# FFN up-projection with the tokens stationary, turned out of PSUM by VectorE; taps and residual sums in other steps

## The chip, the cores and the metric

The program runs on one core of one Trainium2 chip. The metric is the device time of one execution in microseconds (us). The kernel before takes 2447.81 us, the median of three runs (2447.76 to 2447.81).

## The reference, cut to what matters

Two transformer blocks follow each other; the change lies in the feed-forward part of the first. For 256 tokens, D_MODEL 2048 and D_FF 5632, it is

```python
h2 = rmsnorm(x, ffn_norm_w[l])
up = causal_dwconv(h2 @ w_ffn_up[l], conv_w[l], conv_b[l])
a, b = jnp.split(up, 2, axis=-1)
x = x + (jax.nn.silu(a) * b) @ w_ffn_down[l]

def causal_dwconv(u, w, b):          # CONV_WIDTH = 3, along the tokens
    up = jnp.pad(u, ((0, 0), (CONV_WIDTH - 1, 0), (0, 0)))
    y = b
    for j in range(CONV_WIDTH):
        y = y + w[j] * up[:, j:j + S]
    return y
```

The convolution runs along the tokens, feature by feature, and the second product sums over the features.

## The kernel before, in words

All weights come as one stream, w_stream, of some 840 groups in a fixed order. A group is 256 rows by 512 columns of some weight matrix, 512 KB in float32, kept as two 128-row slices of 512 columns. Four slots (RING = 4) hold groups. For each group SP issues a DMA into RAW; ACT copies it rounded into WH ("hi", L1101); DVE subtracts, WL = RAW - WH ("lo", L1605); and PE multiplies. Activations are held as such pairs too, so a product has three terms: hi by hi, lo weight by hi activation, hi weight by lo activation. ACT may write WH of group p+4 when PE has used group p, and SP may refill a slot of RAW when DVE has made its lo.

Each engine's program is written out by hand in the order of the groups. **Step p** on ACT or DVE is: the split of group p+4, then the other work given to that step (`if p == ...`). So the split in step p can begin when PE is through with group p, and everything else that a step holds comes behind its split and ahead of the next.

The feed-forward part takes D_FF in 11 blocks (FB) of 512 features. A block has an "a" tile (its silu branch, 8 groups), a "b" tile (8 groups) and the down-projection of the block before (8 groups, in 4 chunks c of 512 output columns, 2 groups each). The first a and b tiles stand ahead of the loop; the loop over b has 10 passes of 24 groups in the order a, b, down (steps 0 to 23); then come 8 groups of another product (mem1) and the last down-projection.

Up-projection before (`ffn_up`, L876): the weights are the stationary side, 128 columns at a time, and the transposed activations HT (feature rows, hi and lo side by side, 2 x 256 tokens) move. Per group there are 8 matmuls of 512 columns (L892: WH against hi and lo) and 8 of 256 columns (L897: WL against hi). The result has features on partitions: bank f of PSUM holds 128 features by 256 tokens twice, and the two halves are still to be summed. ACT copies one half to FC (`up_copy`, L1365), DVE adds the other and writes FU (`up_sums`, L1902), behind two zero columns. Then the taps, on DVE: a multiply and add of bias (L1911), two multiply-adds (L1913, L1915), each waiting for the one before through `link`. ACT takes silu of the a tile (L1369); for the b tile DVE multiplies the two (`b_tile`, L1921). ACT and DVE make hi and lo of that product, ACTT (`block_hi`, L1375; `block_lo`, L1927); the down-projection needs them (`ffn_down`, L902; matmuls L919 to L921, 12 of 512 columns per group, tokens stationary, weights moving). DVE adds the down result to X (`down_add`, L1935), two chunks at a time.

In the loop before, DVE runs `b_tile` in steps 0 to 3, `block_lo` in step 4, `up_sums` in steps 7 and 15, the a tile's taps in steps 8 to 11 and `down_add` in steps 20 and 23. The semaphore ffn_free tells PE that half of PSUM (4 banks) is free.

All other dense products use `rows_product` (L632; L642 to L644), 12 matmuls of 512 columns per group with HT or another activation tile stationary.

Of the kernel before, what the change touches and what calls it, by code (L numbers as in the profile page):

```python
# [21 lines left out]
F32 = mybir.dt.float32  # L22
# [7 lines left out]
P = 128  # L30
# [147 lines left out]
def build(nc, x_in, mem_in, w_stream, params, final_w, pos_pack, constants, out):  # L178
    with ExitStack() as ctx:
# [38 lines left out]
        FC = sb("FC", [P, FT, S], F32, at_u1 + 4160)  # L218
        FY = sb("FY", [P, 2, S], F32, at_u1 + 4160 + 4 * KB)
# [87 lines left out]
        ffn_free = sem("ffn_free")  # L307
        ffn_copied = sem("ffn_copied")
        ffn_sum = sem("ffn_sum")
# [316 lines left out]
        def _(pe):  # L626
# [249 lines left out]
            def ffn_up(g, u, j, before=None, products_before=None):  # L876

                half = 4 * (u.base % 2)
                pe.wait_ge(ffn_free, u.count(1))
                for q in range(GD):  # L880
                    if before:
                        before(q)

                    def body(slot):
                        late = q == 0 and products_before is not None
                        for fs in ((2, 3), (0, 1)) if late else (range(FT),):
                            if late and 0 in fs:
                                pe.wait_ge(prod_free, 2 + products_before)
                            for f in fs:
                                for kk in range(GK):  # L890
                                    k = q * GK + kk
                                    pe.matmul(PS[:, half + f, :], WH[:, slot, kk, f * P:(f + 1) * P], HT[:, k, :, :],  # L892
                                              start=k == 0, stop=False, skip_group_check=True)
                            for f in fs:
                                for kk in range(GK):
                                    k = q * GK + kk
                                    ins = pe.matmul(PS[:, half + f, 0:S], WL[:, slot, kk, f * P:(f + 1) * P], HT[:, k, 0, :],  # L897
                                                    start=False, stop=k == KT - 1, skip_group_check=True)
                        return ins
                    group(g, j + q, body)  # L900

            def ffn_down(g, u, j, blk, products_before=None):  # L902

                for c in range(NCH):
                    v = At(u.base + c // 2, u.i, u.per)
                    if c % 2 == 0:
                        pe.wait_ge(ffn_free, v.count(1))
                    if c == 0:
                        pe.wait_ge(ffn_lo, blk.count(1))
                    if c == 1 and products_before:  # L910
                        pe.wait_ge(prod_free, 2 + products_before)
                    for q in range(2):
                        def body(slot):
                            for kk in range(GK):
                                k = q * GK + kk
                                for t in range(T):
                                    hi, lo = ACTT[:, k, 0, t * P:(t + 1) * P], ACTT[:, k, 1, t * P:(t + 1) * P]
                                    o = PS[:, 4 * (v.base % 2) + 2 * (c % 2) + t, :]
# [14 lines left out]
            ffn_up(At(g0), At(0), 0, h2_rest, PROD0["mem1"])  # L933
# [6 lines left out]
            pe.wait_ge(ffn_free, 4 * FB - 1)  # L940
            straight("mem1", 1, GD, MEMT)
            ffn_down(At(GROUP0["ffn_down"]), At(4 * FB - 2), 0, At(FB - 1), PROD0["mem2"])
            pe.wait_ge(ffn_free, 2 + 4 * FB - 1)
# [148 lines left out]
        def _(act):  # L1092
# [267 lines left out]
            def up_copy(u, end, f, tile):  # L1360

                act.wait_ge(group_used, end)
                if tile.per or tile.base >= FT:
                    act.wait_ge(ffn_sum, tile.count(1 - FT))
                act.activation(FC[:, f, :], PS[:, 4 * (u.base % 2) + f, 0:S], ACT.Copy).then_inc(ffn_copied, 1)  # L1365

            def silu(tile, f, blk):
                act.wait_ge(ffn_conv, tile.count(1))
                act.activation(FA[:, f, :], FY[:, f % 2, :], ACT.Silu).then_inc(ffn_silu, 1)  # L1369

            def block_hi(blk, end):
                act.wait_ge(ffn_prod, blk.count(1))
                if end is not None:
                    act.wait_ge(group_used, end)
                act.activation(ACTT[:, :, 0, :], FP[:], ACT.Copy).then_inc(ffn_hi, 1)  # L1375

            g0 = GROUP0["ffn"]
            for p in range(2 * GD):
                if p < 4:
                    transposed("h2", HT, [8 + 2 * p, 9 + 2 * p], "ffn")  # L1380
                split(At(g0), p + RING)
                if p == 7:
                    for f in range(FT):
                        up_copy(At(0), g0 + GD, f, At(f))
                if 9 <= p <= 12:
                    silu(At(p - 9), p - 9, None)
            for f in range(FT):
                up_copy(At(1), g0 + 2 * GD, f, At(FT + f))
            with act.Fori(0, FB - 1) as b:
                g = At(g0 + 2 * GD, b, 3 * GD)  # L1390
                for p in range(3 * GD):
                    split(g, p + RING)
                    if p == 4:
                        block_hi(At(0, b, 1), g.count())
                    if p in (7, 15):
                        for f in range(FT):
                            up_copy(At(2 + p // 8, b, 4), g.count(p + 1), f, At(8 + p // 8 * FT + f, b, 8))
                    if 9 <= p <= 12:
                        silu(At(8 + p - 9, b, 8), p - 9, None)
            for p in range(GD):  # L1400
                g = At(GROUP0["mem1"])
                split(g, p + RING)
                if p == FT:
                    block_hi(At(FB - 1), g.count())
# [192 lines left out]
        def _(dve):  # L1597
# [128 lines left out]
            for s, n in ((head_out, 1), (dist_used, 1), (idx_sum, 1), (ffn_free, 2)):  # L1726
                dve.sem_inc(s, n)
# [170 lines left out]
            def up_sums(u, tile):  # L1898

                for f in range(FT):  # L1900
                    dve.wait_ge(ffn_copied, tile.count(f + 1))
                    dve.tensor_tensor(FU[:, f, 2:S + 2], PS[:, 4 * (u.base % 2) + f, S:2 * S], FC[:, f, :], ALU.add).then_inc(ffn_sum, 1)  # L1902
                dve.wait_ge(ffn_sum, tile.count(FT))
                dve.sem_inc(ffn_free, 1)

            def conv(f, tile, feature, silu_done):

                z, y = FU[:, f, :], FY[:, f % 2, :]
                if silu_done is not None:
                    dve.wait_ge(ffn_silu, silu_done)  # L1910
                link(dve.tensor_scalar(y, z[:, 2:S + 2], par("conv", feature * 4 + 2), par("conv", feature * 4 + 3),  # L1911
                                       ALU.mult, ALU.add))
                link(dve.scalar_tensor_tensor(out=y, in0=z[:, 1:S + 1], scalar=par("conv", feature * 4 + 1), in1=y,  # L1913
                                              op0=ALU.mult, op1=ALU.add))
                dve.scalar_tensor_tensor(out=y, in0=z[:, 0:S], scalar=par("conv", feature * 4), in1=y,  # L1915
# [341 lines left out]
```

## Time and profile before

| what | us |
|---|---|
| median of the runs | 2447.81 |
| the profiled execution, its own time | 2447.53 |
| its span in the profile | 2445.7 |
| PE busy in the span | 2439.2 |
| DVE busy | 1562.2 |
| ACT busy | 1229.8 |

The profile is one execution. The 1.8 us between span and time lie outside what is traced. A matmul's shown duration holds its fill and drain, which overlap the next one's: what counts for pace is the distance between starts. PEld is the load of the stationary side. The granted clock of PE is 1.00 throughout, its upper level of 2.4 GHz.

### The profile page before, as it was taken

To read this page: it belongs to the slowest core of one execution; us is meant where nothing else is said; L and a number is where in the kernel's file an instruction comes from. 1 tells how busy PE (TensorE), PEld (TensorE's weight loads), DVE (VectorE), ACT (ScalarE), POOL (GpSimd) and SP (SyncE) were. 2 spreads that over 40 slices of the span, in tenths; PEclk is the share of its full clock that TensorE was granted. 3 is DMA by queue.
4 is the path that set the end of the run, shared out by engine and by line. 5 is a ranking of instruction groups with operands and counts; after the bars stand their busy time and mean duration, and the time that the engine had idled before them with its cause. 6 is when DMAs were issued, how large, how long until landed. Compare 5 with 4: busy or idle time off the path is not lost.

```text
span 2445.7 us, 35617 instructions
## 1 busy us (share of the span) xinstructions
PE 2439.2 (100%) x11757; PEld 2040.6 (83%) x11757; DVE 1562.2 (64%) x1936; ACT 1229.8 (50%) x1612; POOL 235.6 (10%) x250
## 2 busy tenths in 40 slices
PE   9999999999999999999999999999999999999999
PEld 7888888878888888888888888888887888888887
DVE  5467655587877777777777776454456645555564
ACT  6445454555464444444444445454556555655443
POOL 0022233331000000000000000010101000520000
PEclk9999999999999999999999999999999999999999
DMA  7655555566655555555555566855554545544654
GB/s 268 197 182 178 182 175 172 204 216 224 210 188 179 190 195 190 189 188 189 189 189 189 191 193 208 251 188 168 173 183 160 179 160 180 180 163 156 228 183 163
DMA packets 134820, 464.17 MB, mean 190 GB/s; under 512 B 14545, under 2 KB 21329, under 8 KB 134113
## 3 DMA queue, kind: packets, MB, share of 16 engines
q1 hardware_dynamic: 122464, 443.08, 55.0%
q10 hardware_dynamic: 12256, 20.15, 2.5%
q8 instruction: 44, 0.72, 0.1%
q14 instruction: 24, 0.19, 0.0%
q0 software_dynamic: 32, 0.03, 0.0%
HBM read 455.87 MB, written 7.34 MB: 189 GB/s over the span
## 4 chain that ended last, share of the span: by engine, by line
PE 98%; DVE 1%; issue 0%; ACT 0%; DMA 0%; ACTq 0%; SPq 0%; DVEq 0%
PE PS L642 21%; PE PS L644 21%; PE PS L643 21%; PE PS L892 13%; PE PS L897 7%; PE PS L920 3%; PE PS L919 3%; PE PS L921 3%; PE PS L754 1%; PE PS L683 1%; PE PS L724 1%; PE PS L704 0%; PE PS L732 0%; DMA X<-x_in 0%; PE PS L762 0%
## 5 line engine op out<-in xcount | busy, mean ns | idle before, releaser
L1605 DVE TENSOR_TENSOR WL<-RAW,WH 128x1024 fp32r<-128x1024 f32 x842 | 1058.0, 1260 | 830.9 <-ACT WH L1101 825.3
L1101 ACT ACTIVATE WH<-RAW 128x1024 fp32r<-128x1024 f32 x841 | 889.8, 1060 | 1110.7 <-PE PS L644 728.1
L642 PE MATMUL PS<-WH,HT 128*128 128x512 f32 (+1 forms) x1816 | 719.2, 396 | 0.0
L644 PE MATMUL PS<-WH,HT 128*128 128x512 f32 (+1 forms) x1816 | 706.6, 389 | 0.0
L643 PE MATMUL PS<-WL,HT 128*128 128x512 f32 (+1 forms) x1816 | 705.6, 389 | 0.0
L642 PEld LDWEIGHTS PS<-WH,HT 128*128 128x128 f32 x1816 | 341.1, 188 | 72.1 <-issue 5.1
L644 PEld LDWEIGHTS PS<-WH,HT 128*128 128x128 f32 x1816 | 340.8, 188 | 71.3
L643 PEld LDWEIGHTS PS<-WL,HT 128*128 128x128 f32 x1816 | 341.4, 188 | 67.0
L892 PE MATMUL PS<-HT,WH 128*128 128x512 f32 x1408 | 352.8, 392 | 0.0
L892 PEld LDWEIGHTS PS<-HT,WH 128*128 128x128 f32 x1408 | 253.7, 189 | 45.7
L897 PEld LDWEIGHTS PS<-HT,WL 128*128 128x128 f32 x1408 | 192.2, 190 | 13.8
L897 PE MATMUL PS<-HT,WL 128*128 128x256 f32 x1408 | 196.5, 282 | 0.0
L919 PE MATMUL PS<-WH,ACTT 128*128 128x512 f32 x352 | 137.1, 389 | 0.0
L920 PE MATMUL PS<-WL,ACTT 128*128 128x512 f32 x352 | 137.0, 389 | 0.0
L921 PE MATMUL PS<-WH,ACTT 128*128 128x512 f32 x352 | 136.9, 389 | 0.0
L642 PE MATMUL PS<-WH,U 128*128 128x512 f32 x320 | 129.2, 404 | 0.0
L644 PE MATMUL PS<-WH,U 128*128 128x512 f32 x320 | 125.1, 391 | 0.0
L643 PE MATMUL PS<-WL,U 128*128 128x512 f32 x320 | 124.7, 390 | 0.0
L467 POOL TENSOR_TENSOR MS<-MS,CONST 128x4 f32<-128x4 f32 (+1 forms) x7 | 1.4, 200 | 1045.5 <-ACT PS L1142 778.5
L921 PEld LDWEIGHTS PS<-WH,ACTT 128*128 128x128 f32 x352 | 66.1, 188 | 13.8
L919 PEld LDWEIGHTS PS<-WH,ACTT 128*128 128x128 f32 x352 | 66.1, 188 | 13.5
L920 PEld LDWEIGHTS PS<-WL,ACTT 128*128 128x128 f32 x352 | 66.1, 188 | 13.4
(302 smaller groups left out, 1939.3 us busy)
## 6 DMA issues: line engine op xcount, KB each, us to landing
RAW<-w_stream SPq DMA_DIRECT2D x841, 512.0 KB, 3.3
bias_scratch<-BE ACTq DMA_DIRECT2D x12, 256.0 KB, 3.8
MEMR<-mem_in ACTq DMA_DIRECT2D x1, 2048.0 KB, 11.5
X<-x_in ACTq DMA_DIRECT2D x4, 512.0 KB, 4.4
x_scratch<-X ACTq DMA_DIRECT2D x4, 512.0 KB, 4.8
X<-x_scratch ACTq DMA_DIRECT2D x1, 2048.0 KB, 9.3
out<-X ACTq DMA_DIRECT2D x8, 256.0 KB, 2.9
X<-x_in SPq DMA_DIRECT2D x3, 512.0 KB, 9.7
```

The lines of the kernel that those rows point to most:

```text
L642: pe.matmul(o, hi, WH[:, slot, kk, 0:cols], start=k == 0, stop=False)
L643: pe.matmul(o, hi, WL[:, slot, kk, 0:cols], start=False, stop=False)
L644: ins = pe.matmul(o, lo, WH[:, slot, kk, 0:cols], start=False, stop=k == nq * GK - 1)
L683: ins = pe.transpose(PS[:, 4 + at % 4, t * P:(t + 1) * P], src[:, t, k * P:(k + 1) * P], ident)
L724: ins = pe.matmul(PS[:, 6, col:col + keys], QKT[0:n, 0, c, t * P:(t + 1) * P], QKT[0:n, 1, c, 0:keys], start=c == 0, stop=c == last)
L892: pe.matmul(PS[:, half + f, :], WH[:, slot, kk, f * P:(f + 1) * P], HT[:, k, :, :], start=k == 0, stop=False, skip_group_check=True)
L897: ins = pe.matmul(PS[:, half + f, 0:S], WL[:, slot, kk, f * P:(f + 1) * P], HT[:, k, 0, :], start=False, stop=k == KT - 1, skip_group_chec ...
L919: pe.matmul(o, hi, WH[:, slot, kk, :], start=k == 0, stop=False)
L920: pe.matmul(o, hi, WL[:, slot, kk, :], start=False, stop=False)
L921: ins = pe.matmul(o, lo, WH[:, slot, kk, :], start=False, stop=k == FT - 1)
L1101: act.activation(WH[:, g.slot(j)], RAW[:, g.slot(j)], ACT.Copy).then_inc(hi_split, 1)
L1605: dve.tensor_tensor(WL[:, s], RAW[:, s], WH[:, s].bitcast(F32), ALU.subtract).then_inc(lo_split, 1)
```

## The change

Up-projection: the tokens (a 128 x 128 piece of HT, hi or lo) become the stationary side and the weights move, 512 columns at a time, 12 matmuls per group, into one bank for each half of the tokens: banks 2 and 3 for an a tile, 0 and 1 for a b tile. The three terms are summed in PSUM. The result has tokens on partitions, and DVE turns it into FU with 16 transposes per tile (`up_turn`), each of 32 partitions by 256 elements, made of 32 x 32 blocks, from partitions 32a to partitions 32c. Step by step, four of them stand in one step.

The first tap and the bias move to ACT (`taps`); two multiply-adds stay on DVE. FY gets a place for each of the 4 feature tiles of 128. `block_hi` and `block_lo` are split in halves; each chunk of the down-projection is added by itself. The last pass is written out behind the loop of 9, with its b tile turned in steps 18, 19, 20 and 22. In the new loop DVE has: turn of the b tile in steps 0 to 3, `gated` (two taps and the product) in 5 to 8, turn of the a tile in 9 to 12, `block_lo` in 13, a tile's taps in 15 to 18, adds in 17, 19, 21 and 23. ACT has `taps` in 4 and 14, `block_hi` in 10, silu in 17 and 19.

The core of the diff:

```diff
-        FC = sb("FC", [P, FT, S], F32, at_u1 + 4160)
-        FY = sb("FY", [P, 2, S], F32, at_u1 + 4160 + 4 * KB)
+        FY = sb("FY", [P, FT, S], F32, at_u1 + 4160)
...
+            def ffn_up(g, u, j, before=None):
+
+                bank = 0 if u.base % 2 else 2
                 for q in range(GD):
...
                     def body(slot):
...
+                        for kk in range(GK):
+                            k = q * GK + kk
+                            for t in range(T):
+                                hi, lo = HT[:, k, 0, t * P:(t + 1) * P], HT[:, k, 1, t * P:(t + 1) * P]
+                                o = PS[:, bank + t, :]
+                                pe.matmul(o, hi, WH[:, slot, kk, :], start=k == 0, stop=False)
+                                pe.matmul(o, hi, WL[:, slot, kk, :], start=False, stop=False)
+                                ins = pe.matmul(o, lo, WH[:, slot, kk, :], start=False, stop=k == KT - 1)
                         return ins
                     group(g, j + q, body)
 
...
+            def ffn_down(g, j, blk, banks, free):
...
                 for c in range(NCH):
...
+                    free(c)
                     for q in range(2):
+                        if c == 0:
+                            pe.wait_ge(ffn_lo, blk.count(q + 1))
...
             with pe.Fori(0, FB - 1) as b:
                 g = At(g0 + 2 * GD, b, 3 * GD)
-                ffn_up(g, At(2, b, 4), 0)
-                ffn_up(g, At(3, b, 4), GD)
-                ffn_down(g, At(4, b, 4), 2 * GD, At(0, b, 1))
...
+                pe.wait_ge(up_turned, At(1, b, 2).count())
+                pe.wait_ge(down_added, At(3, b, 4).count())
+                ffn_up(g, At(2, b, 2), 0)
+                pe.wait_ge(up_turned, At(2, b, 2).count())
+                ffn_up(g, At(3, b, 2), GD)
...
+                def chunk_free(c):
+                    if c == 0:
+                        pe.wait_ge(down_added, At(4, b, 4).count())
+                    elif c == 2:
+                        pe.wait_ge(up_turned, At(3, b, 2).count())
+                    elif c == 3:
+                        pe.wait_ge(down_added, At(5, b, 4).count())
+                ffn_down(g, 2 * GD, At(0, b, 2), (4, 6, 2, 4), chunk_free)
+            pe.wait_ge(up_turned, 2 * FB - 1)
+            pe.wait_ge(down_added, 4 * FB - 1)
...
+
+            def last_free(c):
+                if c == 0:
+                    pe.wait_ge(down_added, 4 * FB)
+                elif c == 1:
+                    pe.wait_ge(up_turned, 2 * FB)
+                elif c == 3:
+                    pe.wait_ge(down_added, 4 * FB + 1)
+            ffn_down(At(GROUP0["ffn_down"]), 0, At(2 * FB - 2), (4, 0, 6, 4), last_free)
+            pe.wait_ge(down_added, 4 * FB + 2)
...
+            def taps(u, feature, blk):
+
+                act.wait_ge(up_turned, u.count(1))
+                if blk is not None:
+                    act.wait_ge(ffn_prod, blk)
+                for f in range(FT):
+                    act.activation(FY[:, f, :], FU[:, f, 2:S + 2], ACT.Identity, scale=par("conv", feature * 4 + (4 * f + 2)),
+                                   bias=par("conv", feature * 4 + (4 * f + 3))).then_inc(ffn_tap, 1)
+
+            def silu(tile, f):
+                act.wait_ge(ffn_conv, tile.count(f + 1))
+                act.activation(FA[:, f, :], FY[:, f, :], ACT.Silu).then_inc(ffn_silu, 1)
+
+            def block_hi(half, n):
+                act.wait_ge(ffn_prod, half.count(n + 1))
+                act.activation(ACTT[:, 2 * n:2 * n + 2, 0, :], FP[:, 2 * n:2 * n + 2], ACT.Copy).then_inc(ffn_hi, 1)
...
                 for p in range(3 * GD):
                     split(g, p + RING)
                     if p == 4:
-                        block_hi(At(0, b, 1), g.count())
...
+                        taps(At(1, b, 2), b * FT + NFT // 2, None)
+                    if p == 10:
+                        act.wait_ge(group_used, g.count())
+                        block_hi(At(0, b, 2), 0)
+                        block_hi(At(0, b, 2), 1)
+                    if p == 14:
+                        taps(At(2, b, 2), b * FT + FT, At(2, b, 2).count())
+                    if p in (17, 19):
+                        for f in (p - 17, p - 16):
+                            silu(At(2 * FT, b, 2 * FT), f)
+                    if last and p == 3 * GD - 1:
+                        taps(At(3, b, 2), b * FT + NFT // 2 + FT, None)
+            with act.Fori(0, FB - 2) as b:
+                block(b, False)
+            block(FB - 2, True)
...
+            def up_turn(u, end, parts):
+
+                dve.wait_ge(group_used, end)
+                bank = 0 if u.base % 2 else 2
+                for a in parts:
+                    for c in range(4):
+                        src = PS[32 * a:32 * a + 32, bank:bank + 2, :].rearrange("p t (f d) -> p t f d", f=FT)[:, :, :, 32 * c:32 * c + 32]
+                        dst = FU[32 * c:32 * c + 32, :, 2:S + 2].rearrange("p f (t s) -> p t f s", t=T)[:, :, :, 32 * a:32 * a + 32]
+                        ins = dve.transpose(dst, src)
+                if 3 in parts:
+                    ins.then_inc(up_turned, 1)
+
+            def conv(f, tile, feature):
...
+                z, y = FU[:, f, :], FY[:, f, :]
+                dve.wait_ge(ffn_tap, tile.count(f + 1))
+                link(dve.scalar_tensor_tensor(out=y, in0=z[:, 1:S + 1], scalar=par("conv", feature * 4 + (4 * f + 1)), in1=y,
                                               op0=ALU.mult, op1=ALU.add))
-                dve.scalar_tensor_tensor(out=y, in0=z[:, 0:S], scalar=par("conv", feature * 4), in1=y,
+                dve.scalar_tensor_tensor(out=y, in0=z[:, 0:S], scalar=par("conv", feature * 4 + 4 * f), in1=y,
                                          op0=ALU.mult, op1=ALU.add).then_inc(ffn_conv, 1)
 
...
+            def gated(f, tile, feature, silu_done):
+                conv(f, tile, feature)
+                dve.wait_ge(ffn_conv, tile.count(f + 1))
+                dve.wait_ge(ffn_silu, silu_done)
+                ins = dve.tensor_tensor(FP[:, f, :], FA[:, f, :], FY[:, f, :], ALU.mult)
+                if f % 2:
                     ins.then_inc(ffn_prod, 1)
...
+            def block_lo(half, n):
+                dve.wait_ge(ffn_hi, half.count(n + 1))
+                dve.tensor_tensor(ACTT[:, 2 * n:2 * n + 2, 1, :], FP[:, 2 * n:2 * n + 2], ACTT[:, 2 * n:2 * n + 2, 0, :].bitcast(F32),
+                                  ALU.subtract).then_inc(ffn_lo, 1)
+
+            def down_add(c, bank, end):
 
...
+                o = X[:, :, c * CH:(c + 1) * CH]
+                dve.tensor_tensor(o, PS[:, bank:bank + 2, :], o, ALU.add).then_inc(down_added, 1)
...
+            def block(b, last):
                 g = At(g0 + 2 * GD, b, 3 * GD)
                 for p in range(3 * GD):
                     split(g, p + RING)
...
+                    if p < 4:
+                        up_turn(At(1, b, 2), g.count(), (p,))
+                    if 5 <= p < 9:
+                        gated(p - 5, At(FT, b, 2 * FT), b * FT + NFT // 2, At(FT, b, FT).count())
+                    if 9 <= p < 13:
+                        up_turn(At(2, b, 2), g.count(GD), (p - 9,))
+                    if p == 13:
+                        block_lo(At(0, b, 2), 0)
+                        block_lo(At(0, b, 2), 1)
+                    if 15 <= p < (17 if last else 19):
+                        for f in (2 * p - 30, 2 * p - 29) if last else (p - 15,):
+                            conv(f, At(2 * FT, b, 2 * FT), b * FT + FT)
+                    if p in (17, 19, 21, 23):
+                        c = (p - 17) // 2
+                        down_add(c, (4, 6, 2, 4)[c], g.count(2 * GD + 2 * c + 2))
+                    if last and p in (18, 19, 20, 22):
+                        dve.wait_ge(ffn_conv, At(3 * FT, b, 2 * FT).count())
+                        up_turn(At(3, b, 2), g.count(2 * GD), ((18, 19, 20, 22).index(p),))
+            with dve.Fori(0, FB - 2) as b:
+                ch.enter(b, 2 * FT)
+                block(b, False)
+            ch.leave(FB - 2)
+            block(FB - 2, True)
...
+                if p < 4:
+                    gated(p, At(2 * FT * FB - FT), NFT - FT, FB * FT)
+                if p == 5:
+                    block_lo(At(2 * FB - 2), 0)
+                    block_lo(At(2 * FB - 2), 1)
...
+                if p % 2:
+                    down_add(p // 2, (4, 0, 6, 4)[p // 2], GROUP0["ffn_down"] + p + 1)
+            dve.wait_ge(down_added, 4 + 4 * FB)
```

Order on PE, a group of the up-projection in the loop (HT: activations, WH and WL: weights). Before:

```order
L629 ISA [waits ffn_free]
L892 MATMUL PS<-HT,WH 128x512 [waits lo_split]
L892 MATMUL PS<-HT,WH 128x512 x7
L897 MATMUL PS<-HT,WL 128x256 x8
L629 REGISTER_ALU
```

Now, the same place, the loop's first group (and the end of its 12 matmuls):

```order
L928 ISA [waits up_turned]
L628 ISA [waits down_added]
L888 MATMUL PS<-WH,HT 128x512 [waits lo_split]
L889 MATMUL PS<-WL,HT 128x512
L890 MATMUL PS<-WH,HT 128x512
L888 MATMUL PS<-WH,HT 128x512
L889 MATMUL PS<-WL,HT 128x512
L890 MATMUL PS<-WH,HT 128x512
```

Sixteen matmuls became twelve, and the wait for PSUM now names the turn of the tile and the single adds.

Order on DVE at the head of the loop. Before, steps 0 and the split of step 1 (FY and FP: conv output and gated product):

```order
L1605 TENSOR_TENSOR WL<-RAW,WH 128x1024 [waits hi_split]
L1910 ISA
L1911 ISA [waits ffn_silu]
L1911 ISA
L1911 TENSOR_SCALAR FY<-FU,PARAM 128x256
L168 ISA
L1913 ISA [waits dve_chain]
L1913 SCALAR_TENSOR_TENSOR FY<-FU,PARAM,FY 128x256
L168 REGISTER_ALU
L1915 ISA [waits dve_chain]
L1915 SCALAR_TENSOR_TENSOR FY<-FU,PARAM,FY 128x256
```

Now, steps 2 to 5 of the loop:

```order
L1626 TENSOR_TENSOR WL<-RAW,WH 128x1024 [waits hi_split]
L1927 STREAM_TRANSPOSE FU<-PS 32x2x4x32 [waits group_used]
L1927 STREAM_TRANSPOSE FU<-PS 32x2x4x32 x3
L1624 REGISTER_ALU
L1626 TENSOR_TENSOR WL<-RAW,WH 128x1024 [waits hi_split]
L1927 STREAM_TRANSPOSE FU<-PS 32x2x4x32 [waits group_used]
L1927 STREAM_TRANSPOSE FU<-PS 32x2x4x32 x3
L1624 REGISTER_ALU
L1626 TENSOR_TENSOR WL<-RAW,WH 128x1024 [waits hi_split]
L1624 REGISTER_ALU
L1626 TENSOR_TENSOR WL<-RAW,WH 128x1024 [waits hi_split]
L1934 ISA
```

The turn stands where the gated product stood; the gated product comes five steps later.

Order on DVE around the lo half of ACTT, now: end of the a tile's turn (step 12) and step 13.

```order
L1626 TENSOR_TENSOR WL<-RAW,WH 128x1024 [waits hi_split]
L1927 STREAM_TRANSPOSE FU<-PS 32x2x4x32 [waits group_used]
L1927 STREAM_TRANSPOSE FU<-PS 32x2x4x32 x3
L1624 REGISTER_ALU
L1626 TENSOR_TENSOR WL<-RAW,WH 128x1024 [waits hi_split]
L1949 ISA
L1950 TENSOR_TENSOR ACTT<-FP,ACTT 128x2x256 [waits ffn_hi]
L1949 REGISTER_ALU
L1950 TENSOR_TENSOR ACTT<-FP,ACTT 128x2x256 [waits ffn_hi]
```

`block_lo` moved from step 4 to step 13, three groups ahead of the down-projection's first group, 16.

## Rows read from the trace of the kernel before

**Rows 1.** The page, busy time of each engine

```profile
PE 2439.2 (100%) x11757; PEld 2040.6 (83%) x11757; DVE 1562.2 (64%) x1936; ACT 1229.8 (50%) x1612; POOL 235.6 (10%) x250
```

**Rows 2.** Waits of PE, whole span: total us, times, longest

```profile
PE PS L776 <- DVE U L1716: 1.5, 1, 1.5
PE PS L683 <- DMA X<-x_in: 1.3, 1, 1.3
```

**Rows 3.** Windows: 8 down groups, 16 up groups, 16 groups of rows_product

```profile
1019.96:1041.75 21.79, 21.79 (x99) 18.03 (x97) 13.29 (x14) 9.58 (x12) 0.00 (x0) 1.00 0.54 182
1041.75:1086.41 44.66, 44.66 (x257) 39.31 (x256) 35.77 (x51) 20.72 (x25) 0.00 (x0) 1.00 0.59 192
1531.18:1574.70 43.52, 43.52 (x193) 36.05 (x192) 19.61 (x16) 18.79 (x18) 0.00 (x0) 1.00 0.90 260
```

**Rows 4.** Timeline of PE: start us, us, line; L919 begins a group

```profile
1000.41 2.00 PE L892 MATMUL PS<-HT,WH 128*128 128x512 f32 x8
1002.25 1.12 PE L897 MATMUL PS<-HT,WL 128*128 128x256 f32 x8
1003.20 2.00 PE L892 MATMUL PS<-HT,WH 128*128 128x512 f32 x8
...
1091.88 0.39 PE L919 MATMUL PS<-WH,ACTT 128*128 128x512 f32 x1
```

**Rows 5.** Timeline of ACT and DVE, the splits after that matmul

```profile
1092.08 1.06 ACT L1101 ACTIVATE WH<-RAW 128x1024 fp32r<-128x1024 f32 x1 [1.66 <-PE PS L921]
```
```profile
1093.17 1.23 DVE L1605 TENSOR_TENSOR WL<-RAW,WH 128x1024 fp32r<-128x1024 f32 x1 [1.46 <-ACT WH L1101]
```

**Rows 6.** The transposes of this kernel on DVE: duration ns min/median/max

```profile
L1685 DVE STREAM_TRANSPOSE QKT<-QK x128: 292/303/308, 144.0 to 311.0; 32x128 f32<-32x128 f32 x128
```
```profile
L1870 DVE STREAM_TRANSPOSE MEMX<-MEMR x16: 1225/1236/1241, 634.4 to 675.7; 32x1024 f32<-32x1024 f32 x16
```

**Rows 7.** Timeline of DVE around transposes and around `up_sums`

```profile
144.01 5.04 DVE L1685 STREAM_TRANSPOSE QKT<-QK 32x128 f32<-32x128 f32 x16
...
635.97 1.23 DVE L1605 TENSOR_TENSOR WL<-RAW,WH 128x1024 fp32r<-128x1024 f32 x1 [0.35 <-ACT WH L1101]
637.22 1.23 DVE L1870 STREAM_TRANSPOSE MEMX<-MEMR 32x1024 f32<-32x1024 f32 x1
...
1066.51 1.41 DVE L1902 TENSOR_TENSOR FU<-PS,FC 128x256 f32<-128x256 f32 x4
```

**Rows 8.** Timeline of DVE, the loop's first step

```profile
1043.04 1.23 DVE L1605 TENSOR_TENSOR WL<-RAW,WH 128x1024 fp32r<-128x1024 f32 x1 [1.50 <-ACT WH L1101]
1044.18 2.35 DVE L1935 TENSOR_TENSOR X<-PS,X 128x1024 f32<-128x1024 f32 x2
1046.45 1.21 DVE L1605 TENSOR_TENSOR WL<-RAW,WH 128x1024 fp32r<-128x1024 f32 x1
1047.58 0.41 DVE L1911 TENSOR_SCALAR FY<-FU,PARAM 128x256 f32<-128x256 f32 x1
1048.14 0.48 DVE L1913 SCALAR_TENSOR_TENSOR FY<-FU,PARAM,FY 128x256 f32<-128x256 f32 x1 [0.15 <-DVE FY L1911]
1048.78 0.48 DVE L1915 SCALAR_TENSOR_TENSOR FY<-FU,PARAM,FY 128x256 f32<-128x256 f32 x1 [0.15 <-DVE FY L1913]
1049.30 0.43 DVE L1921 TENSOR_TENSOR FP<-FA,FY 128x256 f32<-128x256 f32 x1
1049.64 1.22 DVE L1605 TENSOR_TENSOR WL<-RAW,WH 128x1024 fp32r<-128x1024 f32 x1
```

**Rows 9.** Groups by line, 729 to 1417 us: busy us, mean ns

```profile
L1902 DVE TENSOR_TENSOR FU<-PS,FC 128x256 f32<-128x256 f32 x84 | 29.6, 414 | 0.0
...
L1921 DVE TENSOR_TENSOR FP<-FA,FY 128x256 f32<-128x256 f32 x40 | 17.0, 425 | 1.4
L1927 DVE TENSOR_TENSOR ACTT<-FP,ACTT 128x1024 fp32r<-128x1024 f32 x10 | 12.3, 1226 | 0.7
```

**Rows 10.** Timeline of ACT: two copies of 256 with a scale column

```profile
679.36 0.89 ACT L1346 ACTIVATE MEMT<-MEMX,PARAM 128x256 fp32r<-128x256 f32 x2
```

**Rows 11.** DMA issues: KB each, us from issue to landing

```profile
RAW<-w_stream SPq DMA_DIRECT2D x841, 512.0 KB, 3.3
```

More of the change, by code:

```diff
@@ L306, in build @@
         prod_free = sem("prod_free")
-        ffn_free = sem("ffn_free")
-        ffn_copied = sem("ffn_copied")
-        ffn_sum = sem("ffn_sum")
+        up_turned = sem("up_turned")
+        down_added = sem("down_added")
+        ffn_tap = sem("ffn_tap")
         ffn_conv = sem("ffn_conv")
@@ L884, in body @@
                     def body(slot):
[L885 to L898, printed above, removed]
+                        for kk in range(GK):
[6 more added lines that the diff above has]
+                                ins = pe.matmul(o, lo, WH[:, slot, kk, :], start=False, stop=k == KT - 1)
@@ L1357, in _ @@
                     transposed("h2", HT, [2 * p - 8, 2 * p - 7], "ffn")
[L1360 to L1375, printed above, removed]
+            def taps(u, feature, blk):
[11 more added lines that the diff above has]
+                act.activation(ACTT[:, 2 * n:2 * n + 2, 0, :], FP[:, 2 * n:2 * n + 2], ACT.Copy).then_inc(ffn_hi, 1)
             g0 = GROUP0["ffn"]
@@ L1381, in _ @@
                 split(At(g0), p + RING)
[L1382 to L1389, printed above, removed]
+                if p == 13:
+                    taps(At(0), 0, None)
+                if p == 15:
+                    silu(At(0), 0)
+                    silu(At(0), 1)
+            silu(At(0), 2)
+            silu(At(0), 3)
+            def block(b, last):
                 g = At(g0 + 2 * GD, b, 3 * GD)
@@ L1725, in _ @@
                 dve.tensor_tensor(ident[own, own], col[own], row[own], ALU.is_equal).then_inc(ident_made, 1)
-            for s, n in ((head_out, 1), (dist_used, 1), (idx_sum, 1), (ffn_free, 2)):
+            for s, n in ((head_out, 1), (dist_used, 1), (idx_sum, 1), (down_added, 4)):
                 dve.sem_inc(s, n)
@@ L1895, in _ @@
                     transposed("h2", HT, [2 * p - 8, 2 * p - 7], "ffn")
[L1898 to L1913, printed above, removed]
+            def up_turn(u, end, parts):
[8 more added lines that the diff above has]
+                    ins.then_inc(up_turned, 1)
@@ L1916, in conv @@
                                          op0=ALU.mult, op1=ALU.add).then_inc(ffn_conv, 1)
-            def b_tile(f, tile, feature, silu_done):
-                conv(f, tile, feature, silu_done)
-                dve.wait_ge(ffn_conv, tile.count(1))
-                ins = dve.tensor_tensor(FP[:, f, :], FA[:, f, :], FY[:, f % 2, :], ALU.mult)
-                if f == FT - 1:
-                    ins.then_inc(ffn_prod, 1)
-            def block_lo(blk):
-                dve.wait_ge(ffn_hi, blk.count(1))
-                dve.tensor_tensor(ACTT[:, :, 1, :], FP[:], ACTT[:, :, 0, :].bitcast(F32), ALU.subtract).then_inc(ffn_lo, 1)
@@ L1929, in down_add @@
-            def down_add(u, end):
-                dve.wait_ge(group_used, end)
-                half, c0 = 4 * (u.base % 2), 2 * (u.base % 2)
-                for c in range(2):
-                    o = X[:, :, (c0 + c) * CH:(c0 + c + 1) * CH]
-                    ins = dve.tensor_tensor(o, PS[:, half + 2 * c:half + 2 * c + 2, :], o, ALU.add)
-                ins.then_inc(ffn_free, 1)
+            def gated(f, tile, feature, silu_done):
[4 more added lines that the diff above has]
+                if f % 2:
+                    ins.then_inc(ffn_prod, 1)
@@ L1942, in _, with block @@
                 split(At(g0), p + RING)
-                if p == 7:
-                    up_sums(At(0), At(0))
-                if 8 <= p <= 11:
-                    f = p - 8
-                    conv(f, At(f), f, f - 1 if f >= 2 else None)
-            up_sums(At(1), At(FT))
-            with dve.Fori(0, FB - 1) as b:
-                ch.enter(b, 2 * 2 * FT)
+                if 8 <= p < 12:
+                    up_turn(At(0), g0 + GD, (p - 8,))
+                if p in (14, 15):
+                    for f in (2 * p - 28, 2 * p - 27):
+                        conv(f, At(0), 0)
+            def block(b, last):
                 g = At(g0 + 2 * GD, b, 3 * GD)
```

54 lines of the change are left out of this document (8 added, 46 removed).

## The prediction

> **What bounds the kernel now.** First the page's busy times: PE 2439.2 us of a span of 2445.7, every other engine far below [rows 1]. A busy PE could still be a slow one, so next PE's waits: two, of 1.5 and 1.3 us, in the whole span [rows 2]. So the time is the pace at which PE takes groups, and nothing else counts until it makes PE wait. Then the windows: 8 down groups take 21.79 us, 2.724 each; 16 groups of `rows_product` take 43.52, 2.720 each; 16 up groups take 44.66, 2.791 each [rows 3]. All three kinds move the same 6144 columns per group; the up groups do it in 16 matmuls, the others in 12. The timeline shows where the extra goes: 8 matmuls of 512 columns take 1.84 us from first start to the next line's (1000.41 to 1002.25), 0.230 each, and 8 of 256 take 0.95 (to 1003.20), 0.119 each [rows 4]. A matmul of 256 columns costs more than half of one of 512, the 0.227 of the 12 in 2.72. Last I read DVE and ACT around the splits, since the change puts its new work there.
>
> **The change on PE.** Each up group becomes 12 matmuls of 512 columns with a piece of HT stationary, the very form of `rows_product`. For a pair of up tiles (16 groups) that is 44.66 - 43.52 = 1.14 us less; for 11 blocks 12.5 us. The first tile's 16 transposes of the normalised rows stay. The removed ffn_free waits cost nothing before and give nothing.
>
> **The change on DVE.** Here lies the risk. Splits keep a clock: after a group ends on PE and the next begins (L919 at 1091.88, 2 x 2.72 after the first at 1086.41), ACT's split starts 0.20 us later and DVE's 1.29 us later, and what follows it on DVE starts 1.14 after that [rows 4, 5, 8]. A step has 2.72 us.
>
> How long is a transpose of 32 x 256 out of PSUM? No row has it. From SBUF, 128 elements take 303 ns and 1024 take 1236 [rows 6], 1.041 ns per element, so 256 take 303 + 133 = 436. Sixteen of 128 elements take 5.04 us [rows 7]: (5.04 - 0.30)/15 = 0.316 from start to start, 13 ns more than one lasts. Four `up_sums` additions of 128 x 256, one operand in PSUM, take 1.41 with 0.414 for one [rows 7, 9], so 0.332 apart: these overlap, the transposes do not. PSUM as a source costs the additions nothing against SBUF (414 against 425 ns) [rows 9]. So I take 0.449 us per transpose. Bounds: 0.332 apart if they overlapped as the additions do; 0.632, twice the 128-element pace, if the fixed part grew too. The first transpose behind a split also starts 1.25 after it, not 1.14 (635.97 to 637.22) [rows 7], in three of four cases where it reads other partitions than the last.
>
> The Trainium skill says the same of this trace and speaks against the change (VectorE: DVE Perf Modes, Two Vector instructions with no wait between them): an instruction whose output starts in another quadrant of 32 partitions than the last one's is held until all earlier ones are through. By that rule all four transposes of a step but at most one are held, so the overlap of the additions is not to be hoped for; the trace agrees with its 0.316 against 0.303.
>
> A turn step costs 1.14 + 0.11 + 4 x 0.449 = 3.05, 0.33 over the step (0.22 in the first); four put DVE 1.2 behind. In step 4 ACT needs the finished turn: it starts its four taps at 1.29 + 1.2 = 2.5, they take 4 x 0.40 = 1.6 (the pair with a scale takes 0.89 [rows 10], one of them 0.49), and the next split's hi comes 1.09 later: DVE goes on at 5.2 where 4.0 was due, again 1.2 behind. `gated` takes the steps' split 1.14, then 0.64, 0.52 and 0.34 [rows 8], 2.64 in all, so four steps win back 0.3; the second turn adds 1.2: 2.1 behind at step 13. There, after its split, DVE makes the first half of ACTT's lo, 128x512: 1.23 less 512 elements, 0.69. It is ready at 1.29 + 2.1 + 1.14 + 0.69 = 5.2 after group 13 ended. PE wants it for group 16, 2 x 2.72 = 5.44 after, and its weight load some 0.2 sooner. **So the wait that is late next is ffn_lo at group 16, and it is met with 0 to 0.2 us to spare.** Other deadlines are far: a lo split is wanted 3 x 2.72 = 8.2 after group p ends and is ready at 2.5 plus the lag; RAW's load takes 3.3 [rows 11] after that split and is wanted 10.9 + 0.2 after.
>
> Over a block DVE needs 24 x 1.14 + 32 x 0.449 + 0.7 (held starts) + 4 x 1.5 (gated) + 4 x 1.12 (taps of a: 0.64 + 0.48) + 1.2 (lo) + 4 x 1.13 (adds; 2.27 for two [rows 8]) = 58.7 of 65.3 us. It fits, and steps 14 on clear the lag: 14 holds a split alone, and a step with taps of a takes 1.14 + 1.12 = 2.3. The worst later step, 19 of the last pass (split, add, turn, 4.2), adds 1.5 where 5 are free.
>
> The rest at nothing: `up_copy` leaves ACT (4 per tile), `taps` comes; halves for wholes in `block_hi` and `block_lo` add one instruction's fixed part each; single adds bring chunk 0's banks back sooner. The cover is ACT's half-idle time and the slack above; if step 4's cover were gone it would show at ffn_lo. The last pass written out costs PE nothing, as PE keeps its loop. Ahead of the first pass DVE has two double-tap steps (14 and 15, 3.1 us each), which brings about 0.7 us of lag into it, and so up to 0.7 us of stall once. I charge 0.7.
>
> **The sum.** 2447.53 - 12.5 + 0.7 = 2435.7 for the profiled execution; the median before stands 0.3 above that execution, so 2436.0.
>
> **Rivals.**
> A, the turn is dearer out of PSUM and PE stalls at group 16. A block has 32 transposes ahead of that deadline, so each 0.01 us on one is 0.32 on the lag, less 0.1 spare, times 10 passes. At 0.06 more the stall is 1.8 per pass: 2436 + 18 = 2454, slower than before. Gain and loss meet at 0.04 more (0.490); slower by over 0.2% starts at about 0.506. At the bound 0.632 it is 5.8 per pass, 2494. For it: no row transposes out of PSUM, and the argument is a chain of terms with nothing to spare. Against: the additions show no charge for PSUM.
> B, a mild form: 0.46 to 0.475, 2438 to 2443.
> C, the pace of PE does not change: the columns stay at 6144 per group, and if these alone set the pace, the change gives next to nothing, 2447. Against it: the 0.119 for 256 columns and the 2.720 of `rows_product` with the same HT stationary, in this very trace [rows 3, 4].
> The Trainium skill gives the isolated gap between matmuls as N/2.4 + 2.5 ns (TensorE: Matmul & The Clock Gate, Back-to-back issue gap). By an estimate from that page 16 matmuls take 2.600 us and 12 take 2.590, so the change would give 1.8 us, 2446. The trace's 0.227 and 0.119 lie above that rule by 11 and 10 ns, so a matmul saved is worth more here.
>
> **How the numbers follow.** A change below 0.2% (4.9 us) can't be told from none. Forecast, 2434.5 to 2438: 0.59. B: 0.15. Between B and the slower side (0.475 to 0.506 per transpose, 2443 to 2452): 0.11. C: 0.03. A beyond that: 0.12. Faster 0.74, same 0.14, slower 0.12. The range: down to 2434.0, if nothing stalls and the first block is smooth; up to 2447, which leaves out most of A and the last part of the middle case, some 0.17.
>
> **What would show it.** PE's line for the up-projection with 2112 matmuls, 16 groups in 43.5 us; the transposes at 436 ns and a step's four 1.8 us apart; in the waits of PE, ffn_lo's maker (DVE, ACTT) with nothing or tenths per pass. If that row shows over 1 us a pass the forecast is wrong, by the transpose's price or by `taps` (more than 0.40 apart, or a table load on ACT). If 16 groups take more than 44 without waits, C holds.

## The result, and the profile after

The changed kernel takes 2451.36 us (median of 20 runs, 2449.34 to 2452.32); the kernel before, run beside it, 2447.66 (2447.36 to 2448.59). The ratio is 1.0015, 95% interval 1.0009 to 1.0021: 3.7 us slower, where 2436.0 was forecast and 2447 was the upper end. By the 0.2% bound of the prediction that is the case "same"; the interval shows it slower all the same. The profiled execution took 2452.02 us, its span is 2450.2. The 20 executions fall apart by PE's mean granted clock: two with 1.00 took 2449.3 and 2449.5, fourteen with 0.999 took 2451.0 to 2452.0, four with 0.998 took 2452.1 to 2452.3. So up to 3 us go with the clock, whose fall is shown below, and without it the kernel would still be 1.8 slower than before.

The page after, busy time of each engine, and the waits of PE (total us, times, longest):

```profile
PE 2432.1 (99%) x11053; PEld 2005.1 (82%) x11053; DVE 1655.1 (68%) x2123; ACT 1244.7 (51%) x1623; POOL 235.6 (10%) x250
```

```profile
PE PS L908 <- DVE ACTT L1950: 11.1, 10, 3.4
...
PE PS L641 <- issue: 0.5, 1, 0.5
```

Where PE had two waits, 2.8 us together [rows 2], it now has, beside such two, ten on the lo half of ACTT, one per pass, and one ahead of mem1. A steady pass in windows: 8 down groups, 16 up groups, and what PE loses. Columns as in [rows 3]: the window, its us, busy us and count of PE, PEld, DVE, ACT and POOL, then the granted clock, the share of the DMA engines, GB/s.

```profile
957.45:979.35 21.90, 21.90 (x96) 18.12 (x97) 18.06 (x21) 9.94 (x13) 0.00 (x0) 1.00 0.65 215
979.35:1022.88 43.53, 43.53 (x193) 35.85 (x191) 38.32 (x60) 20.65 (x24) 0.00 (x0) 1.00 0.55 180
1022.88:1023.97 1.09, 0.15 (x1) 0.01 (x1) 1.09 (x3) 1.09 (x3) 0.00 (x0) 1.00 0.02 8
```

The 16 up groups take 43.53 us where they took 44.66 [rows 3], as forecast. Then PE stands for 1.09, and the down groups take 0.11 more than their 21.79, which is the restart. So a pass takes 66.52 against 66.45 before: the gain of each pass is spent in it.

The timeline of DVE shows how the lateness is built (steps 3 to 5, then 12 and 13). Below, the lag of a step is how much later its split starts on DVE than at PE's pace of 2.72 us per step:

```profile
992.50 1.22 DVE L1626 TENSOR_TENSOR WL<-RAW,WH 128x1024 fp32r<-128x1024 f32 x1
993.76 1.85 DVE L1927 STREAM_TRANSPOSE FU<-PS 32x256 f32<-32x256 f32 x4
995.64 1.23 DVE L1626 TENSOR_TENSOR WL<-RAW,WH 128x1024 fp32r<-128x1024 f32 x1
998.93 1.23 DVE L1626 TENSOR_TENSOR WL<-RAW,WH 128x1024 fp32r<-128x1024 f32 x1 [2.06 <-ACT WH L1111]
...
1018.76 1.23 DVE L1626 TENSOR_TENSOR WL<-RAW,WH 128x1024 fp32r<-128x1024 f32 x1
1020.02 1.85 DVE L1927 STREAM_TRANSPOSE FU<-PS 32x256 f32<-32x256 f32 x4
1021.91 1.23 DVE L1626 TENSOR_TENSOR WL<-RAW,WH 128x1024 fp32r<-128x1024 f32 x1
1023.05 1.29 DVE L1950 TENSOR_TENSOR ACTT<-FP,ACTT 128x512 fp32r<-128x512 f32 x2
```

and ACT beside it, in step 4:

```profile
995.86 2.08 ACT L1376 ACTIVATE FY<-FU,PARAM 128x256 f32<-128x256 f32 x4 [1.65 <-DVE FU L1927]
997.85 2.00 ACT L1111 ACTIVATE WH<-RAW 128x1024 fp32r<-128x1024 f32 x2
```

The pass's first split, step 0, starts at 983.37, and step p is due 2.72 x p later. Step 4 starts 1.39 late (995.64 for 994.25). Then DVE stands idle for 2.06, though it is behind: ACT began its four taps 0.25 after the turn ended, they take 2.0, and only then comes the hi split that DVE's step 5 needs. Step 5 is 1.96 late, step 9 1.67, step 13 3.18 (1021.91 for 1018.73). The first half of lo ends near 1023.74; PE's matmul starts at 1023.97, due at 1022.88.

The first pass is worse. The timeline of PE there, and two windows with its granted clock:

```profile
821.88 0.79 PE L908 MATMUL PS<-WH,ACTT 128*128 128x512 f32 x1 [3.36 <-DVE ACTT L1950]
822.47 0.63 PE L909 MATMUL PS<-WL,ACTT 128*128 128x512 f32 x1
822.90 0.63 PE L910 MATMUL PS<-WH,ACTT 128*128 128x512 f32 x1
...
827.16 0.48 PE L908 MATMUL PS<-WH,ACTT 128*128 128x512 f32 x1
```

```profile
820.00:822.00 2.00, 0.12 (x1) 0.12 (x1) 2.00 (x3) 1.96 (x4) 0.00 (x0) 0.63 0.35 141
822.00:824.00 2.00, 2.00 (x5) 1.61 (x6) 2.00 (x3) 1.06 (x2) 0.00 (x0) 0.50 0.75 256
```

PE stands 3.5 us (due 818.36), its clock falls to 0.50, the 1.2 GHz level, and 12 matmuls start 0.43 apart instead of 0.227, from 821.88 to 827.16, before it is back: 2.6 us more.

The account: 11 pairs of tiles at 43.53 for 44.66 give 12.4. The first pass loses 3.5 + 2.6; eight passes lose about 1.2 each, 9.6; the last pass 0.5 (0.4 to its first down matmul, 0.1 restart); the wait ahead of mem1 0.7. Together 16.9 - 12.4 = 4.5, and the spans differ by 4.5.

### The profile page after: what moved, and what is told of

Same layout as the page of the kernel before. It is cut to its first block, busy times and chain, and to the rows that moved or that the text cites. A ratio compares the mean times of both kernels' runs of the same rounds, so it can differ in the third digit from the quotient of the medians.

```text
span 2450.2 us, 34145 instructions
## 1 busy us (share of the span) xinstructions
PE 2432.1 (99%) x11053; PEld 2005.1 (82%) x11053; DVE 1655.1 (68%) x2123; ACT 1244.7 (51%) x1623; POOL 235.6 (10%) x250
## 4 chain that ended last, share of the span: by engine, by line
PE 81%; DVE 10%; issue 7%; ACT 2%; DVEq 0%; DMA 0%; ACTq 0%; SPq 0%
PE PS L641 21%; PE PS L643 21%; PE PS L642 21%; DVE FU L1927 5%; PE PS L908 3%; PE PS L910 3%; PE PS L909 3%; DVE WL L1626 2%; ACT WH L1111 1%; DVE FY L1937 1%; DVE FY L1935 1%; PE PS L890 1%; PE PS L888 1%; PE PS L889 1%; PE PS L753 1%
## 5 line engine op out<-in xcount | busy, mean ns | idle before, releaser
L641 PEld LDWEIGHTS PS<-WH,HT 128*128 128x128 f32 x1816 | 341.1, 188 | 71.8 <-issue 4.9
L643 PEld LDWEIGHTS PS<-WH,HT 128*128 128x128 f32 x1816 | 340.9, 188 | 71.5
L642 PEld LDWEIGHTS PS<-WL,HT 128*128 128x128 f32 x1816 | 341.3, 188 | 66.9
L888 PE MATMUL PS<-WH,HT 128*128 128x512 f32 x704 | 274.3, 390 | 0.0
L890 PE MATMUL PS<-WH,HT 128*128 128x512 f32 x704 | 273.9, 389 | 0.0
L889 PE MATMUL PS<-WL,HT 128*128 128x512 f32 x704 | 273.9, 389 | 0.0
L1927 DVE STREAM_TRANSPOSE FU<-PS 32x256 f32<-32x256 f32 x352 | 156.9, 446 | 5.9
L890 PEld LDWEIGHTS PS<-WH,HT 128*128 128x128 f32 x704 | 132.1, 188 | 27.5
L889 PEld LDWEIGHTS PS<-WL,HT 128*128 128x128 f32 x704 | 132.2, 188 | 27.4
L888 PEld LDWEIGHTS PS<-WH,HT 128*128 128x128 f32 x704 | 132.1, 188 | 27.2
L908 PE MATMUL PS<-WH,ACTT 128*128 128x512 f32 x352 | 139.2, 395 | 11.1 <-DVE ACTT L1950 11.1
```

Source lines behind the costliest of these rows:

```text
L641: pe.matmul(o, hi, WH[:, slot, kk, 0:cols], start=k == 0, stop=False)
L642: pe.matmul(o, hi, WL[:, slot, kk, 0:cols], start=False, stop=False)
L643: ins = pe.matmul(o, lo, WH[:, slot, kk, 0:cols], start=False, stop=k == nq * GK - 1)
L888: pe.matmul(o, hi, WH[:, slot, kk, :], start=k == 0, stop=False)
L889: pe.matmul(o, hi, WL[:, slot, kk, :], start=False, stop=False)
L890: ins = pe.matmul(o, lo, WH[:, slot, kk, :], start=False, stop=k == KT - 1)
```

## The experiments

All are timed against the kernel before on the same chip. Theory 1: a late deadline, ffn_lo at group 16, turns lag of DVE into idle PE. Theory 2: DVE is short of time in the pass as a whole. Theory 3: transposes alone, or taps alone, make the lag. The edits of the first six are to the changed kernel's loop. The diffs are shortened; `...` and `par(...)` stand for what is left out.

**The lo half two steps earlier.**

```diff
-                    if p == 13:
+                    if p == 11:            # ahead of that step's up_turn
                         block_lo(At(0, b, 2), 0)
                         block_lo(At(0, b, 2), 1)
```

> The kernel after the change with one edit: DVE makes the lo half of ACTT in step 11, ahead of that step's transposes, not in step 13. Work and count of instructions stay the same. Theory 1 (a late deadline): PE stalls only because ffn_lo comes behind 3.2 us of lag at step 13 (5.5 us in the first pass); made at step 11 it is ready some 6 us before group 16, the stalls of 1.1 us per pass and the 3.5 us of the first pass with its 12 slow matmuls go, and the time is 2435 (2434 to 2437). Theory 2 (DVE is short of time): the lag itself is the trouble, and PE then waits for lo splits instead; 2446 to 2451.

Measured: 2438.66 us (2438.46 to 2439.75), ratio to before 0.9965 (0.9951 to 0.9978). PE's waits:

```profile
PE PS L641 <- issue: 1.9, 1, 1.9
...
PE PS L908 <- DVE WL L1626: 0.6, 1, 0.6
```

The ten waits on ACTT are gone, with the work of DVE unchanged (busy 1653.1 us, 1655.1 before the edit), so theory 2 falls. The time is above the 2434 to 2437 that theory 1 named, because the lag itself is still there: in the first pass it now reaches the split of group 16 (0.6), and in the last pass the add that frees the banks of mem1 (1.9).

**The b tile's taps one per step.**

```diff
-                    if p == 4:
-                        taps(At(1, b, 2), b * FT + NFT // 2, None)
+                    if 4 <= p < 8:         # tap of feature tile p - 4 only
+                        taps(At(1, b, 2), b * FT + NFT // 2, None, (p - 4,))
```

> The kernel after the change with one edit: ACT makes the four taps of the b tile one per step in steps 4 to 7, not all in step 4. Theory 1: the next hi split then waits for one tap (0.5 us) instead of four (2.0), DVE goes on 1.5 us sooner in step 5, and the lag at step 13 falls from 3.2 to 1.7, so that ffn_lo is in time in all passes but the first, where 2.0 of 3.5 us stay: 2437.5 to 2439.5. Theory 3 (the transposes alone make the lag, the taps lie beside them): DVE is behind by its own work anyhow, and the time stays at 2450 to 2451.

Measured: 2438.37 us (2438.27 to 2439.43), ratio 0.9964 (0.9950 to 0.9977). As theory 1 had it: one wait on ACTT is left, 1.9 us, in the first pass (2.0 were expected). DVE's idle time ahead of step 5 fell from 2.06 to 0.58 in this row:

```profile
991.32 1.23 DVE L1626 TENSOR_TENSOR WL<-RAW,WH 128x1024 fp32r<-128x1024 f32 x1 [0.58 <-ACT WH L1111]
```

No instruction became shorter and none went away. The 13.0 us under the changed kernel come from this alone, that the four no longer stand together ahead of a split.

**Transposes that stay in their partitions.**

```diff
-  dst = FU[32 * c:32 * c + 32, ...][:, :, :, 32 * a:32 * a + 32]
+  dst = FU[32 * a:32 * a + 32, ...][:, :, :, 32 * c:32 * c + 32]
```

> The kernel after the change with one edit: the four transposes of a step write into the same 32 partitions that they read, so the blocks land in wrong places of FU; count and sizes are the same. It measures whether the 0.45 us from start to start is the price of a change of partitions. If an instruction that keeps to the last one's partitions overlaps it as the additions of 128x256 do, starts are 0.35 to 0.37 apart, a step with a turn takes 2.6 to 2.7 us, the lag at step 13 is under 1 us in the steady passes, and the time is 2435 to 2436. If transposes never overlap, the starts stay 0.45 apart and the time 2451.

The values are wrong in this kernel, since the blocks stand in wrong places. Measured: 2435.38 us (2434.97 to 2435.56), ratio 0.9950 (0.9937 to 0.9964). Its timeline of DVE, beside 1.85 for four in the rows above:

```profile
984.77 1.49 DVE L1927 STREAM_TRANSPOSE FU<-PS 32x256 f32<-32x256 f32 x4
```

With the last at about 0.40, starts are (1.49 - 0.40)/3 = 0.36 apart, against (1.85 - 0.45)/3 = 0.47 (0.45 in the first step's 1.80). So the change of partitions costs about 0.1 us per transpose, and without it a step with a turn takes 2.78 us, almost the 2.72 it has. The Trainium skill's rule says that an instruction is held until all earlier ones are through when its output starts in another quadrant of 32 partitions than the last output (VectorE: DVE Perf Modes, Two Vector instructions with no wait between them). The trace agrees: 0.47 apart with that change, 0.36 without it.

Spreading the taps, or taking the change of partitions out, removes the steady stall each by itself: theory 3 falls in either form. The lag is their sum, and PE pays only what lies above some 2.1 us.

**Taps without the bias column.**

```diff
- act.activation(FY[:, f, :], ..., ACT.Identity, scale=par(...), bias=par(...))
+ act.activation(FY[:, f, :], ..., ACT.Copy, scale=par(...))
```

> The kernel after the change with one edit: the taps on ACT are a Copy with the scale column alone; the convolution's bias is left out. It sizes the second column: with it a tap lasts 0.59 us, and four take 2.0; the nearest row of before, with a scale column alone, is 0.49, 0.40 apart. Theory 1: four taps take 1.6, DVE's step 5 comes 0.4 sooner, each pass stalls 0.4 less: 2446 to 2448. If the length is that of reading FU and not of the second column, nothing changes: 2451.

Measured: 2446.59 us (2444.81 to 2448.40), ratio 0.9996 (0.9987 to 1.0005). A tap lasts 495 ns where it lasted 588, and four take 1.71 where they took 2.08:

```profile
L1376 ACT ACTIVATE FY<-FU,PARAM x88: 491/495/515, 770.9 to 1443.6; 128x256 f32<-128x256 f32 x88
```

```profile
1021.26 0.49 PE L908 MATMUL PS<-WH,ACTT 128*128 128x512 f32 x1 [0.47 <-DVE ACTT L1949]
1087.29 0.49 PE L908 MATMUL PS<-WH,ACTT 128*128 128x512 f32 x1 [0.47 <-DVE ACTT L1949]
```

The pass is 66.03, 0.47 less, near the 0.4 expected. DVE's step 5 comes 0.46 sooner after step 4 (2.83 for 3.29): 0.38 by the taps' length, 0.08 by their earlier start. So the lag reaches PE one for one. This sizes the tap, the term that was taken too small; but with taps of the forecast length PE's down matmul still starts 0.63 late in each pass, so the tap's size is only part of the miss. The edit also takes Copy for Identity, and no run tells that from the column. Against the function as the cause: an Exp of 128x256 with one parameter column lasts 493 in the trace of before (L1171), like this Copy.

**Both schedule edits.** Diff: the first two together.

> Both edits at once: lo half of ACTT in step 11, and the b tile's taps one per step. Theory 1: nothing is late any more in the steady passes either way, so it adds to the first edit only what is left in the first pass, under 1 us: 2434 to 2436, the best of all. Theory 2 (DVE is short of time): taking 1.5 us of lag away helps where moving the deadline did not; it would be clearly faster than the first edit alone.

Measured: 2436.21 us (2436.16 to 2436.35), ratio 0.9953 (0.9939 to 0.9967). No wait on ACTT or on a down group's split is left; 0.9 stays ahead of mem1. It is 2.5 under the first edit alone, where theory 1 had named under 1, without the wait ahead of mem1. Theory 2 named a clear gain, but the place is another: what shrank, 0.6 to nothing and 1.9 to 0.9, are single events at the two ends of the loop.

**The lo half one step later.**

```diff
-                    if p == 13:
+                    if p == 14:
```

> The kernel after the change with one edit the other way: the lo half of ACTT one step later, in step 14 behind another split. Theory 1: it is ready 1.14 us later in every one of the 10 passes, so PE stalls 2.2 us instead of 1.1: 2451.4 + 11.4 = 2463, and more if PE's granted clock falls after each stall as it did after the 3.5 us of the first pass (2.4 us for 12 slow matmuls): up to 2485. Theory 2: the time is set by DVE's work, which is the same: 2451 to 2453.

Measured: 2467.91 us (2467.76 to 2468.24), ratio 1.0083 (1.0068 to 1.0097). PE waits 22.4 us in ten times where it waited 11.1, 1.13 more per pass, as 1.14 was worked out. That is 11.3 of the 16.6 over the changed kernel. Most of the rest is the clock, within the 2463 to 2485 that theory 1 named: of eight passes that wait 2.05 to 2.09, five take 67.6 and three, in which the clock falls, 69.2, together 4.8 more:

```profile
960.78 0.49 PE L908 MATMUL PS<-WH,ACTT 128*128 128x512 f32 x1 [2.06 <-DVE ACTT L1950]
1028.42 0.49 PE L908 MATMUL PS<-WH,ACTT 128*128 128x512 f32 x1 [2.07 <-DVE ACTT L1950]
1097.68 0.49 PE L908 MATMUL PS<-WH,ACTT 128*128 128x512 f32 x1 [2.09 <-DVE ACTT L1950]
```

```profile
956.00:966.00 10.00, 7.94 (x36) 6.25 (x35) 8.17 (x12) 5.15 (x7) 0.00 (x0) 1.00 0.66 208
1023.00:1036.00 13.00, 10.93 (x41) 8.55 (x40) 9.41 (x15) 5.36 (x8) 0.00 (x0) 0.87 0.52 163
```

From 1028.42 to 1097.68 are 69.26 us, 1.6 more than the pass ahead of it.

**The first a tile's work one step sooner, ahead of the loop (told in words).**

```diff
-   ACT: p == 13: taps;  p == 15: silu 0, 1;  behind the steps: silu 2, 3
+   ACT: p == 12: taps;  p == 14: silu 0, 1;  p == 15: silu 2, 3
-   DVE: p in (14, 15): two convolutions each
+   DVE: p in (13, 14)
```

> The kernel after the change with its first a tile's taps, convolution and silu one step earlier on ACT and DVE ahead of the loop (taps in step 12, convolution in 13 and 14, silu in 14 and 15, none behind step 15). It tests what the first pass costs. Theory 1: DVE enters the loop 2.2 us behind because step 15 and the silus behind it end late; with step 15 left for the split alone it enters 0.5 to 1 behind, the first pass stalls 1.5 to 2 us instead of 3.5, and if a stall that short leaves PE's granted clock up, its 12 slow matmuls (0.43 against 0.23 us, 2.4 in all) go too: 2451.4 - 1.8 - 2.4 = 2447, or 2449.5 if the clock still falls. The other passes stay at 66.50 us. Rival: the first pass is late for another reason, and it stays at 2451.

Measured: 2450.04 us (2448.74 to 2450.46), ratio 1.0009 (1.0000 to 1.0018). That is above both values that theory 1 named (2447 and 2449.5) and under the rival's 2451. The sum was off, the cause is borne out in the profiled execution (2448.98 us): the first pass waits 2.18 instead of 3.36, the clock stays at 1.00, and that pass, from one last up matmul to the next, takes 67.77 us instead of 71.48, while the others stay at 66.53. The value of 2447 took 1.8 off for the stall, where 1.2 went, and 2.4 for the clock, of which the median execution had lost only some 1.9 (2451.36 against 2449.4). The executions lie in two groups: three with a mean granted clock of 1.00 take 2448.7 to 2449.1, eight with 0.999 take 2449.8 to 2450.5. So in most of them the clock still falls somewhere, though the wait is shorter; where in the span is not seen, since one execution is profiled.

**The best version.** The fifth experiment with that prelude and the last pass rearranged (told in words):

```diff
-   last pass, up_turn of the b tile in steps 18, 19, 20, 22; its taps in step 23
+   in steps 18, 20, 22, 23; its taps one per step in mem1's steps 0 to 3
-   mem1: gated products in steps 0 to 3, block_hi in 4, block_lo in 5
+   gated products in 1 to 4, both in 5
```

> Both edits of the fifth experiment and that prelude, and in the last pass the b tile's turn in steps 18, 20, 22 and 23 instead of 18, 19, 20 and 22, with its taps one per step in mem1's steps 0 to 3, its gated products in 1 to 4 and both halves of ACTT in 5. In the fifth experiment PE still waits 0.95 us ahead of mem1, for the add of chunk 2, which the turn in step 19 holds back. Theory 1: that wait goes, and nothing else is late: span 2433.4, 2435.2 by the runs, 1.0 under the fifth experiment.

Measured: 2435.04 us (2434.75 to 2436.82), ratio 0.9950 (0.9936 to 0.9963), span 2433.4. The wait ahead of mem1 is gone. It beats the kernel before by 12.6 us and the changed one by 16.3. Its span is 12.3 under before's, which is the gain on PE and nothing lost.

## Why the prediction was wrong, point by point

**What bounds the kernel, and PE's pace.** Right. 1.13 us per pair of tiles, 1.14 forecast; the best version has the whole 12.3 of the 12.5.

**The price of a transpose out of PSUM.** Nearly right: 445 ns (median of 352) for 436, PSUM for almost nothing, no overlap, 0.45 to 0.47 apart for 0.449. The turn steps took 12.27 in all for 12.1, and the second turn, whose first transpose also started 1.24 after its split and not 1.14, 12.39. Together that is 0.5 us of lag more than I had, 0.1 from that start and the rest from a hundredth or so per transpose.

**The taps. This step failed.** By the prediction "they take 4 x 0.40 = 1.6" and DVE is "again 1.2 behind". The row was a Copy with one column of parameters; the tap has two, scale and bias, and lasts 588 ns, 0.50 apart, 2.0 in all. With the 0.25 from the turn's end to the first tap, which I had not counted, step 5's lag is 0.57 above step 4's, where I had no more. The prediction named taps more than 0.40 apart as a way to be wrong, but gave them no price and no chance. The fourth experiment shows the second column's part, 0.09 per tap and 0.47 per pass. The Trainium skill has the figure (ScalarE: Activation LUTs, What ACT_TABLE_LOAD costs, on the time of an ACTIVATE): 186 ns and 0.833 ns per element, and about 93 ns for each pointer column. An estimate from that page is 585 ns for two columns; the trace agrees with 588, and with 495 for one.

**The deadline.** Right in place, wrong in size: ffn_lo at group 16 was named as the next late wait, "met with 0 to 0.2 us to spare". It was missed by 1.1, since the lag at step 13 was 3.18 for the forecast 2.1; 0.57 of that is the step with the taps, 0.5 the two turns, and both went one way. The tap's size alone does not account for it: with taps of the forecast length the kernel still took 2446.59, at the upper end of the range. A margin of a tenth at the end of a sum of ten terms, counted ten times over, should have been forecast as a stall with a wide range, not as none.

**The first pass.** Charged 0.7, cost 6.1, of which 1.2 is what every pass lost. I counted DVE's two double steps but not ACT, where a table load of 1.28 and four silus that wait for DVE hold up the hi splits; DVE entered the loop 2.3 late (split of step 0 at 781.14, 778.85 by PE's pace) and was 5.6 behind at step 13. And I gave no price to the clock.

**"Other deadlines are far."** Wrong in the last pass: there the add of chunk 2 in step 21 frees the banks of mem1, and the turn in step 19 held it back, 0.5 in the changed kernel and up to 1.9 once the stall ahead of it was gone. The eighth experiment removes it.

**The rivals.** A had the mechanism, the stall at group 16, but drove it by the transposes' price alone; its place was right and its point of decision (0.506 per transpose) was not reached. B had a price of 0.46 to 0.475, and the measured spacing lies at its lower edge; by its own sum that alone makes 2438. The rest is the taps and the first pass, and no rival had these. The deadline sees only the lag: 0.1 us more on each of four taps is as much of it as 0.012 more on each of 32 transposes. C is refuted: the 16 up groups take 43.53.

## What to carry to other kernels

Where an engine works by steps behind another, list for each wait the lag at which it becomes late, not the engine's load over the loop: here DVE had 9 of 66.5 us free per pass and still stopped PE in each. A block of small instructions that stands ahead of what the next engine waits for delays that engine by its whole length: DVE stood idle for 2.06 us behind four taps together, and for 0.58 with one per step, which PE did not notice in the steady passes. A slow lead-in and a wait of a few us cost more than they last when PE's clock falls behind them.

## What the runs showed of the hardware that was not expected

In the profiled executions PE's granted clock fell to its 1.2 GHz level behind waits of 3.36 us (changed kernel, 12 slow matmuls), 2.69 (taps without the bias column, 8) and 4.50 (lo half one step later, 8). In the last of these it also fell behind three of eight waits of 2.05 to 2.09 us. It did not fall behind 2.18 in the prelude's experiment, nor behind 1.87 and 1.88 in the first two. An activation of 128x256 with one parameter column lasts 495 ns and with two 588. A transpose of 32x256 costs 0.36 us from start to start where it stays in its 32 partitions and 0.45 to 0.47 where it does not.
